# Gate logs, gate sums and late attention units reordered, and the first gate projection of the merge moved into the mixers' tail, in a four-layer hybrid network

## What is computed

```python
for layer in range(2):
    u = rms_norm(h, norm_mix_g[layer])
    p_a, p_b, p_c, p_gate = split(u @ w_in[layer])
    y_a = rwkv7_branch(p_a, ...)      # 8 heads of 64, a delta-rule state
    y_b = hgrn2_branch(p_b, ...)      # 4 heads of 128, gated state with lower bounds
    y_c = dsa_branch(p_c, cos, sin)   # 8 heads of 64, attention over the 64 best keys
    branch = einsum('bsnc,ncd->bsnd', stack([y_a, y_b, y_c]), w_branch[layer])
    gates = sigmoid(p_gate)           # 3 x 1024 columns
    merged = sum(gates * branch, axis=branches)
    h = h + merged @ w_o[layer]
    h = h + conv_glu(rms_norm(h, norm_ffn_g[layer]), w_up, conv_w, conv_b, w_down)
```

## Time and profile before

| | |
|---|---|
| median of three runs | 1979.3 us |
| profiled execution, its own time | 1983.01 us |
| its span | 1981.2 us |
| TensorE busy | 1869.6 us (94%) |
| VectorE busy | 1317.3 us (66%) |
| ScalarE busy | 1082.4 us (55%) |
| GpSimd busy | 923.7 us (47%) |
| mean granted TensorE clock | 0.960 |

### The profile page before, as it was taken

The page is one execution under the profiler, slowest core; times in us unless marked ns, Lnnn a source line. Parts: engine busy times, 40 slices in busy tenths (PEclk is TensorE's granted clock), DMA queues, the critical chain, the costliest instruction groups (busy, mean ns, idle before and its releaser), DMA issues.

```text
span 1981.2 us, 43199 instructions
## 1 busy us (share of the span) xinstructions
PE 1869.6 (94%) x15850; PEld 1742.0 (88%) x15850; DVE 1317.3 (66%) x1956; ACT 1082.4 (55%) x1862; POOL 923.7 (47%) x662
## 2 busy tenths in 40 slices
PE   9988889999999988989999999987999999879999
PEld 9968779999999968879999999865999997669999
DVE  4677725669955587735669964676886527768754
ACT  5653455557655643455457664646555446365543
POOL 5732449929986633359929985521000044120000
PEclk9999989999999999899999999977999999779999
DMA  7522015656666522015556665320566653116664
GB/s 244 155 87 65 13 35 168 176 155 186 187 206 176 158 86 71 23 40 169 176 155 186 187 195 169 112 80 17 164 186 201 186 157 116 59 38 171 187 186 144
DMA packets 146917, 271.13 MB, mean 137 GB/s; under 512 B 16433, under 2 KB 16946, under 8 KB 146738
## 3 DMA queue, kind: packets, MB, share of 16 engines
q1 hardware_dynamic: 145296, 264.97, 45.8%
q10 hardware_dynamic: 1442, 3.66, 0.5%
HBM read 267.52 MB, written 1.05 MB: 136 GB/s over the span
## 4 chain that ended last, share of the span: by engine, by line
PE 66%; DVE 19%; POOL 7%; ACT 6%; issue 2%; DVEq 0%; DMA 0%; ACTq 0%
PE bank L669 66%; POOL ring_split L1361 7%; ACT arena L1395 5%; DVE arena L1957 1%; DVE arena L1956 1%; PE bank L811 1%; DVE ring_split L2075 1%; DVE arena L2537 1%; DVE arena L2144 1%; DVE arena L2518 1%; DVE arena L2294 0%; DVE arena L2559 0%; ACT hi_ring L1395 0%; DVE arena L2191 0%; DVE arena L2597 0%
## 5 line engine op out<-in xcount | busy, mean ns | idle before, releaser
L1361 POOL TENSOR_TENSOR ring_split<-ring,hi_ring 128x512 fp32r<-128x512 f32 x602 | 856.1, 1457 | 742.0 <-ACT hi_ring L1395 741.4
L1395 ACT ACTIVATE hi_ring<-ring 128x512 fp32r<-128x512 f32 x890 | 537.5, 628 | 410.3 <-PE bank L669 388.4
L669 PE MATMUL bank<-u_hi,hi_ring 128*128 128x256 f32 (+1 forms) x2160 | 615.6, 285 | 6.8 <-POOL ring_split L1361 6.6
L669 PE MATMUL bank<-u_split,hi_ring 128*128 128x256 f32 (+1 forms) x2160 | 607.9, 281 | 0.0
L669 PE MATMUL bank<-u_hi,ring_split 128*128 128x256 f32 (+1 forms) x2160 | 607.0, 281 | 0.0
L669 PEld LDWEIGHTS bank<-u_hi,hi_ring 128*128 128x128 f32 (+1 forms) x2160 | 407.0, 188 | 13.5 <-POOL ring_split L1361 6.8
L669 PEld LDWEIGHTS bank<-u_split,hi_ring 128*128 128x128 f32 (+1 forms) x2160 | 406.8, 188 | 1.7
L669 PEld LDWEIGHTS bank<-u_hi,ring_split 128*128 128x128 f32 (+1 forms) x2160 | 406.3, 188 | 1.0
L669 PE MATMUL bank<-arena 64*64 64x64 f32 (+6 forms) x3680 | 240.7, 256 | 27.4 <-DVE arena L2191 18.6
L669 PEld LDWEIGHTS bank<-arena 64*64 64x64 f32 (+3 forms) x3680 | 210.3, 156 | 63.3 <-issue 39.6
L2075 DVE TENSOR_TENSOR ring_split<-ring,hi_ring 128x512 fp32r<-128x512 f32 x288 | 196.5, 712 | 93.1 <-ACT hi_ring L1395 90.4
(11 more groups left out here) (265 smaller groups left out, 2522.3 us busy)
## 6 DMA issues: line engine op xcount, KB each, us to landing
ring<-in_stream SPq DMA_DIRECT2D x1002, 256.0 KB, 2.7
par<-in_params ACTq DMA_DIRECT2D x3, 637.0 KB, 4.1
h<-in_x SPq DMA_DIRECT2D x4, 256.0 KB, 4.1
cst<-in_cst SPq DMA_DIRECT2D x1, 993.0 KB
out<-h ACTq DMA_DIRECT2D x3, 256.0 KB, 2.6
par<-in_params ACTq DMA_DIRECT2D x1, 633.0 KB, 8.5
out<-h ACTq DMA_DIRECT2D x2, 128.0 KB, 2.2
msk<-in_masks SPq DMA_DIRECT2D x1, 104.0 KB
```

Of the source, the lines that this page charges most:

```text
L669: ins = nc.tensor.matmul(o, l, r, start=start, stop=stop)
L1361: G.tensor_tensor(ring_lo[:, c, :], ring[:, c, :], hi_ring[:, s % HI_RING, :].bitcast(F32), ALU.subtract).then_inc(lo_by_pool, 1)
L1395: return nc.scalar.activation(o, i, f, **kw)
```

## The change

It does three things, in the layers of the first kind alone.

- `gate_logs` is cut in two: the three tensor operations stay where they were, the eight tensor_scalar go behind VectorE's level 1. `gate_sums` is cut in two: the sum and the four tensor_scalar stay behind the rotation of Rq0, the eight scans go behind VectorE's level 2.
- On TensorE `logits(4)` and `logits(5)` go ahead, each in front of a transpose that it stood behind; on VectorE `probabilities(2)` goes ahead of `masked_logits(3)`; on ScalarE `softmax(4)` goes ahead of `take_values(2)`.
- G02 is projected right behind `logits(4)`, ahead of the transpose of unit 2. ScalarE copies it to a new buffer `gate_raw` of 128x512, and the sigmoid reads that. GpSimd writes its four low halves between `level_operands` 1 and 2. The list of banks follows.

```diff
-    g += ["S14", "S15", f"CL{a3}", "S16", "S17", "H3", f"CP{a2}", "R1", f"CO{a2}", f"CL{a4}", f"CP{a3}", "H4", "SA1", f"CO{a3}", f"CL{a5}", f"CP{a4}", "H5"]
+    g += ["S14", "S15", f"CL{a3}", "S16", "S17", "H3", f"CL{a4}", MERGE[0][0], f"CP{a2}", "R1", f"CO{a2}", f"CL{a5}", f"CP{a3}", "H4", "SA1", f"CO{a3}", f"CP{a4}", "H5"]
...
-    g += ["HO0", "HO1", "GM0", "GM1", MERGE[0][0], "HN0", "HN1", "GV0", "GV1"]
+    g += ["HO0", "HO1", "GM0", "GM1", "HN0", "HN1", "GV0", "GV1"]
...
+        gate_raw = cv(512)
...
                 hgrn_pairs(3)
+                logits(4)
+                project(MERGE[0][0], 2, u_parts)
                 turn_probs(2)
                 right_sides(1)
                 values(2)
-                logits(4)
+                logits(5)
                 turn_probs(3)
                 hgrn_pairs(4)
                 solutions(1)
                 values(3)
-                logits(5)
                 turn_probs(4)
...
-                project(MERGE[0][0], 2, u_parts)
                 pe.wait_ge(S["hosq_ready"], past["hosq_ready"] + 2)
...
                 for k in range(LEVELS):
                     level_operands(B, past, k)
+                    if k == 1:
+                        low_parts(done, stage_ends[1 + l][MERGE[0][0]])
+                        done = stage_ends[1 + l][MERGE[0][0]]
...
                 pair_decays(4)
                 take_turned(2)
+                bank = B.wait(act, MERGE[0][0])
+                C.link(A(gate_raw, bank[:, :], ACT.Copy))
+                B.release(act, MERGE[0][0])
                 take_sides(1)
+                softmax(4)
                 take_values(2)
                 pair_decays(5)
                 take_turned(3)
-                softmax(4)
                 take_solutions(1)
...
-                    bank = B.wait(act, n)
+                    bank = B.wait(act, n) if i else gate_raw
...
                 scores(1)
-                gate_logs()
+                gate_logs_first()
                 for k in range(1, LEVELS):
                     take_scores(0, pair_of(k))
                     for c in range(2):
                         level(c, k, 0)
                         level(c, k, 1)
                     if k == 1:
+                        gate_logs_rest()
                         rotate("Rq0", 0, 2)
-                        gate_sums()
+                        gate_sums_first()
                     elif k == 2:
+                        gate_sums_rest()
                         rotate("Rq1", 2, 2)
...
                 take_scores(1, (4, 5))
+                probabilities(2)
                 masked_logits(3)
                 take_scores(1, (6, 7))
-                probabilities(2)
                 take_pairs(3)
```

More of the change, by code:

```diff
@@ L1747, in _ @@
                     C.link(A(gate_buf[i % 2], bank[:, :], ACT.Sigmoid), S["gate_ready"])
-                    B.release(act, n)
+                    if i:
+                        B.release(act, n)
                 nc.scalar.preload_act_table_set(LN_EXP)
@@ L2306, in lower_bounds, with gate_logs_first @@
                     C.link(V.tensor_scalar(ln1m, omlb, 2.0 ** -64, None, ALU.max), S["hcol_in"])
-                def gate_logs():
+                def gate_logs_first():
                     dve.wait_ge(S["hcol_out"], past["hcol_out"] + 2)
@@ L2314, in gate_logs, with gate_logs_rest @@
                     C.link(V.tensor_tensor(hks, hls, bf, ALU.subtract))
+                def gate_logs_rest():
                     for j in range(4):
@@ L2319, in gate_logs, with gate_sums_first @@
                     dve.sem_inc(S["lse_in"], 1)
-                def gate_sums():
+                def gate_sums_first():
                     dve.wait_ge(S["lse_out"], past["lse_out"] + 1)
@@ L2326, in gate_sums, with gate_sums_rest @@
                         C.link(V.tensor_scalar(v3(hks, 4)[:, j, :], v3(hks, 4)[:, j, :], omlb[:, j:j + 1], None, ALU.mult))
+                def gate_sums_rest():
                     for i in range(8):
```

## The result

The changed kernel takes **1932.28 us** (median of 4 runs, 1928.77 to 1940.56) against 1980.78 us for the kernel before on the same chip: **ratio 0.9762 [0.9725, 0.9798]**, some 47 us. The same kernel run again later gave 1936.73 us (6 runs, 1931.18 to 1948.95) against 1980.42 us (29 runs, 1965.16 to 1989.41): **0.9789 [0.9746, 0.9832]**, some 42 us.

A forecast was written before the change was run, and what follows sets the result against it. TensorE's own work was taken as two thirds of the span, gains lying in its stalls; behind the tail ScalarE, then GpSimd bound. 11.0 + 16.8 - 4.5 + 5.2 = 28.5 us gained, median 1950.8 us, range 1943 to 1964.

The forecast's parts named there:

- no fall of the clock at all: Rival: TensorE keeps full clock in both layers' tails, 33.0 us gained, 1946.3 us; no chance of its own given.
- part 1: Gate logs and sums moved on VectorE at the pairwise inversion's start: 5.5 us per layer, 11.0 us for two.
- First stall of part 1: Inversion level 1: TensorE's 4.06 us wait for VectorE goes, as the eight gate-log operations move behind that level.
- Second stall: Inversion level 2: with the scans moved, TensorE goes on at 154.0, not 159.71; gain 5.7 us, upper end 7.2.
- Just in time: Rotations behind the moved scans end at 164.4, just when the values projection ends (164.3); 0.2 us taken off per layer.
- Part 2a: GpSimd writes four low halves, 6 us, in idle time behind the operands of level 1; cost 0, at most 1 us.
- Tail without clock: Mixers' tail without a half-clock stretch: 12.0 us gained in the first layer, 4.8 in the second, sum 16.8.
- One fall, 4.5 us: Tail: TensorE drops to 1.2 GHz in one of two layers, costing 4.5 us; likeliest case, chance 0.4.
- The baseline: Second layer's old tail, read from one profile as ending at 870.50 us, giving a gain of 4.8 us there.
- Part 2c: Behind the tail, where ScalarE rules: 2.6 us gained per layer, 5.2 for two; bounds 1.5 and 5.7 us.
- slower: Rival: TensorE stays at 1.2 GHz from gate projection to last values in both layers, 11 us slower, 1990; chance 0.04.

The follow-up runs named there:

- e8: The changed kernel unaltered, run again beside the kernel before: 1936.73 us, ratio 0.9789.
- e4: The changed kernel with 6 tiny VectorE operations ahead of the second kind's first norm, as a delay: 1940.65 us, ratio 0.9825.
- e1: The kernel before with only the gate logs and gate sums reordered, the tail as before: 1973.9 us, ratio 0.9972.
- e3: The kernel before with 11 tiny VectorE operations ahead of the second kind's first norm, as a delay: 1979.82 us, ratio 1.0008.
- e2: The kernel before with only the tail's new order and the moved projection, gate logs and sums as before: 1952.69 us, ratio 0.9886.
- e5: The kernel before with only the projection moved ahead of unit 2's transpose, logits and probabilities in the old order: 1968.87 us, ratio 0.9938.
- e6: The kernel before with only the new order of logits, softmax and probabilities, the projection left behind the tail: 1970.4 us, ratio 0.9945.
- e7: The kernel before with 12 dummy matmuls in the one gap ahead of unit 2's transpose: 1968.81 us, ratio 0.9951.
- e9: The kernel before with the tail's new order and 13 dummy matmuls in the gap, the projection left behind the tail: 1960.45 us, ratio 0.9908.
- v2: The changed kernel with 32 dummy matmuls in the waits of each layer of the second kind: 1938.79 us, ratio 0.9787.
- e10: The kernel before, old order, with dummy matmuls in all four waits of the tail: 1967.99 us, ratio 0.9936.
- e11: The kernel before with only the gate logs cut in two, the sums whole at their old place: 1976.13 us, one execution.
- e12: The kernel before with only the gate sums cut in two, the logs at their old place: 1984.16 us, one execution.

## Why the prediction was wrong

The walks through the two stretches were right in the main, the likeliest case for the clock was not: what came is the rival "no fall of the clock at all" (33.0 us), and more. The miss of 19.1 us between the two profiled executions (47.6 against 28.5) is 1.6 in part 1, 6.2 in the tail (18.5 against 16.8 - 4.5), 0.1 behind it, and 2.5 in D1 and 9.4 in the second kind, both of which the sum left out, less 0.7. Step by step:

- **First stall of part 1.** Right. Gone, as drawn; the eight operations start 0.45 us apart as forecast (0.41 each), and VectorE takes up the sums at 144.95 us (forecast 145.5).
- **Second stall.** The mechanism right, the size a little low: the four tensor_scalar take 5.11 us as forecast, the sum ahead of them 1.37 us, not 2.2, and TensorE goes on at 152.66, not 154.0; 7.05 us for 5.7.
- **"Just in time", the 0.2 us for rotations and scans.** This step failed. Beside GpSimd the last operation of a rotation takes 1.66 us where it took 0.69 in the kernel before; the two rotations take 6.3 us (158.97 to 165.29) where the walk had 4.1, and level 3 gets 1.76 + 1.64 us of waits for 0.32. Some 1.4 us are given back at full clock, and up to 2.7 more by the clock that falls behind the waits. The profile after shows 5.6 and 7.0 us gained because it had no fall in this stage. Over the four executions with the change as it is or part 1 alone (after, e8, e4, e1) I is 64.7 and 63.5 us, over seven without (before, e3, e2, e5, e6, e7, e9) 68.4 and 69.3: **9.5 us for two layers where 11.0 was forecast** (9.7 with v2 and e10 taken in). More of it is the logs' than the sums': alone the ones brought 2.8 and 3.5 us (e11), the others 1.3 and 1.2 (e12).
- **Part 2a.** Right, at no cost: the four low halves took 4.96 us, and the transposes of the next turn wait 1.62 us, as in the earlier trace rows.
- **Tail without clock.** Its terms came out at bank wait 0.24, logits 1.13, projection 5.7, 36 records 4.86, then 4.00, late by 1.56 (forecast 1.0). From the transpose of unit 4 to the end I took 10.9 us from the earlier trace rows and called half a microsecond of it slow clock; at full clock it is 9.4, so 1.5 of it was. 16.8 us forecast, 18.5 measured.
- **"One fall, 4.5 us".** This is the step that failed first. I saw a fall in layer 2 with only 1.62 us in front of it, took it for a thing that strikes one layer in two whatever stands in the gap, and charged it. The term measured 0: none of sixteen tails has a fall, there or elsewhere. The argument wasn't empty, for that fall did come back with the gap filled (e5 and e7, second layer). Why it kept away from the changed kernel isn't shown, and may be luck.
- **The baseline.** For layer 2 I took the 90.87 us of one profile. It was the mildest of ten old tails, whose mean is 96.3. So the tails are worth (96.3 - 85.2) x 2 = 22 us, against 12.3 in the sum. Of the 42 - 28.5 = 13.5 us that the repeated comparison lies above the forecast this is the larger part, 9.9; one profile couldn't show it.
- **Part 2c.** Right: 2.8 and 2.5 us, forecast 2.6 each. ScalarE rules there. In e9, which leaves the projection behind the tail, P is back at 22.8; in e5, which moves it alone, it is 20.1.
- **Left out of the sum.** D1 is anything from 157.9 to 161.7 us, with 157.9 and 160.5 both in kernels with the whole change and without it, which gave 2.5 us here; matmuls start closer together there, and I found no cause. The second kind gave 9.4, of which more than 5 to 6 can hardly be the change's. The sum put both at nothing without a reason.

Without D1 and the second kind the stages say 9.5 + 22 + 5.3 = 37 us; the repeated comparison says 42 with an interval from 33 to 50. Of the case "slower", TensorE at 1.2 GHz all through the tail, no trace of it was seen. My range reached down by the case of no fall and a few us more, and not even by all that its own terms allow: no fall and the 5.7 us end of part 2c make 33.0 + 6.2 = 39.2 us, 1940. It needed the spread of the old tails as well.

**Long waits, or short ones close together.** In the traces the clock fell behind a wait of 2.54 us in e7, and in e8 behind two of 1.75 and 1.64 us. The prediction had drawn on the Trainium skill, TensorE: Matmul & The Clock Gate, section "HAM oscillation — how this bites in real kernels", which is about long waits between bursts; read as a rule about the longest wait, it would have e7 clean, and the trace of e7 doesn't agree (14 and 24 us at 1.2 GHz). The next section of that page of the Trainium skill, "A second HAM failure mode: psum-queue depth-cycling", speaks of frequent short idle times between groups of matmuls. With that the traces of e7 and e8 agree, and so does e10, where filling all four waits left none at 1.2 GHz. The prediction weighed only the first of the two.

## What to carry to other kernels

A gap filled is worth little while its neighbours stay: count the waits of a stretch together, and ask which remain. Where the clock takes part, one profile is one draw: the same work with the same waits had a fall in one execution and none in the next. So read the same stage in several executions, untouched ones too, before taking a baseline or crediting a gain. When work moves on VectorE, price it and whatever it displaces by rows in which GpSimd is as busy as it will be at the new place.

## What the runs showed of the hardware

- TensorE fell to 1.2 GHz behind two waits of 1.75 and 1.64 us with 0.92 us of work between them (e8, first layer, ahead of 169.68 us) and even behind 1.17 and 0.92 us (e8, second layer, ahead of 729.07 us). Waits alone don't decide it: behind the same waits of 0.71, 0.21, 0.92 to 0.95 and 1.62 us it fell in four of eleven tails with the old order and in none of six with the change's.
- The same program on one core spreads by 24 us over 29 executions (1965 to 1989). Between profiles the differences stand mostly where the granted clock is 0.50; a tail at 1.00 repeats between 84.8 and 85.3 us in sixteen layers.
- At a granted clock of 1.00 and with TensorE busy throughout, the same row of matmuls (128x256) started 0.118 us apart in one execution and 0.113 in another (767 and 796 in 90 us), 2.5 us on a stage of 160. What sets it isn't shown.
- On VectorE, beside GpSimd's low halves: tensor_scalar on 128x256 1.24 us for 0.41, eight scans of 128x128 6.30 us for 3.63, tensor_tensor of two SBUF operands on 128x512 1.66 us for 0.69.
- Dummy matmuls kept the clock up and bought time in the waits of the tail (e9, e10); spread over the second kind they bought 48 us less of slow clock and no time at all (v2).
